# Token halves of the decay logs on the partition halves, zeroing in bf16, and a reordered plan in the recurrent mixer of a four-layer model

## What is computed

```
proj = h @ w_in
qp, fp, ip, gp = split(proj)                       # 1024 columns each
log_f = logaddexp(log(lb), log1p(-lb) + log_sigmoid(fp))
k = (1 - lb) * sigmoid(-fp)
q = silu(qp) * 128 ** -0.5
# per head, with b the running sum of log_f over the tokens:
#   o_n = sum over m <= n of (q_n . (exp(b_n - b_m) * k_m)) v_m
o = o * rsqrt(mean(o * o) + eps) * norm_g * sigmoid(gp)
out = o @ w_out
```

## Time and profile before

| | us |
|---|---|
| median of 3 runs | 1396.22 |
| lowest and highest | 1389.8 and 1397.57 |
| the profiled execution | 1391.12 |
| its span, first to last instruction | 1389.3 |
| PE busy in it | 1338.4 (96%) |
| chain that ended last, on PE | 88% |

### The profile page before, as it was taken

One profiled execution on the slowest core, in us unless ns is written; L12 is line 12 of the kernel. 1 busy time (PEld: TensorE's weight loads), 2 busy tenths in 40 slices (PEclk: granted clock), 3 DMA queues, 4 the chain that ended last, 5 costly groups with the idle time before them and its releaser, 6 DMA issues.

```text
span 1389.3 us, 19642 instructions
## 1 busy us (share of the span) xinstructions
PE 1338.4 (96%) x7598; PEld 1098.7 (79%) x7598; DVE 394.4 (28%) x817; ACT 713.0 (51%) x1241; POOL 1044.5 (75%) x875
## 2 busy tenths in 40 slices
PE   6999899999999999999999998899999999899997
PEld 4888788888877777888887777688887788788886
DVE  2156321111156562211104463301103232411112
ACT  6364564454486765544434564444534554444531
POOL 6244878887894637888888776888879977788874
PEclk9799999999999999999999999999999999999999
DMA  8223456665653423655665543466656544465652
GB/s 270 90 77 92 136 166 199 182 192 173 190 169 92 132 77 122 195 184 182 183 194 160 184 135 122 148 214 186 196 175 190 188 144 152 136 214 182 196 170 89
DMA packets 63116, 224.91 MB, mean 162 GB/s; under 512 B 7344, under 2 KB 7984, under 8 KB 63024
## 3 DMA queue, kind: packets, MB, share of 16 engines
q1 hardware_dynamic: 62736, 223.57, 51.6%
q10 hardware_dynamic: 288, 0.10, 0.0%
HBM read 222.59 MB, written 1.05 MB: 161 GB/s over the span
## 4 chain that ended last, share of the span: by engine, by line
PE 88%; POOL 3%; DVE 3%; ACT 3%; DMA 2%; issue 2%; SPq 0%; DVEq 0%; ACTq 0%
PE G L1027 25%; PE G L1028 24%; PE G L1034 24%; POOL wlo L2168 3%; PE A L1206 1%; PE A L1058 1%; ACT whi L1909 1%; PE A L1140 1%; DMA raw<-in_w_e 1%; PE G L1206 1%; PE A L1272 1%; DMA raw<-in_w_b 1%; PE A L1176 1%; DVE X L1416 1%; PE G L1140 1%
## 5 line engine op out<-in xcount | busy, mean ns | idle before, releaser
L2168 POOL TENSOR_TENSOR wlo<-raw,whi 128x256 fp32r<-128x256 f32 (+1 forms) x867 | 1034.8, 1230 | 326.9 <-ACT whi L1909 326.8
L1909 ACT ACTIVATE whi<-raw 128x1024 fp32r<-128x1024 f32 x403 | 425.7, 1060 | 352.8 <-PE G L1034 325.3
L1027 PE MATMUL G<-whi,xh 128*128 128x512 f32 (+2 forms) x1200 | 465.2, 391 | 9.9 <-DVE xl L1391 6.7
L1028 PE MATMUL G<-whi,xl 128*128 128x512 f32 (+2 forms) x1200 | 452.2, 380 | 0.0
L1034 PE MATMUL G<-wlo,xh 128*128 128x512 f32 (+2 forms) x1200 | 353.4, 381 | 1.6 <-POOL wlo L2168 1.4
L1027 PEld LDWEIGHTS G<-whi,xh 128*128 128x128 f32 x1200 | 228.3, 190 | 54.3 <-ACT whi L1909 8.8
L1028 PEld LDWEIGHTS G<-whi,xl 128*128 128x128 f32 x1200 | 228.8, 191 | 37.7
L1034 PEld LDWEIGHTS G<-wlo,xh 128*128 128x128 f32 x1200 | 220.2, 190 | 46.9 <-POOL wlo L2168 3.6
L1027 PE MATMUL G<-whi,hh 128*128 128x512 f32 x352 | 139.5, 396 | 0.0
L1028 PE MATMUL G<-whi,hl 128*128 128x512 f32 x352 | 138.9, 395 | 0.0
L1034 PE MATMUL G<-wlo,hh 128*128 128x512 f32 x352 | 110.5, 395 | 0.0
(11 more groups left out here) (360 smaller groups left out, 1183.9 us busy)
## 6 DMA issues: line engine op xcount, KB each, us to landing
raw<-in_g SPq DMA_DIRECT2D x88, 512.0 KB, 4.0
raw<-in_u SPq DMA_DIRECT2D x88, 512.0 KB, 4.0
raw<-in_d SPq DMA_DIRECT2D x88, 512.0 KB, 4.2
raw<-in_w_h SPq DMA_DIRECT2D x32, 512.0 KB, 3.6
raw<-in_w_e SPq DMA_DIRECT2D x24, 512.0 KB, 3.8
raw<-in_w_a SPq DMA_DIRECT2D x24, 512.0 KB, 3.6
...
```

What stands on the lines that cost most here:

```text
L1027: e.matmul(o, sh[:, kt, xs], whi[h][:, ws], start=u.first and j == 0, stop=False)
L1028: e.matmul(o, sl[:, kt, xs], whi[h][:, ws], start=False, stop=False)
L1909: e.activation(whi[c % NH][:, 0:n], raw[c % NR][:, 0:n], ACT.Copy).then_inc(s_hi, 1)
L2168: m = e.tensor_tensor(wlo[c % NH][:, i:j], raw[c % NR][:, i:j], whi[c % NH][:, i:j].bitcast(F), ALU.subtract)
```

## The change

**Layout of the logs.** `lfh` and `lfl` become `lf[0]` and `lf[1]`, one for each half of 64 of the 128 tokens. The high part of a token half stays on its own 64 partitions, the low part goes to the other 64. One matmul then contracts high and low part together, but of one token half only. `Wr` keeps its 1152 columns and holds for each token half the three blocks that need whole 128 columns, and, shared by both, the 64-column pieces of the six finer levels. H1 for t = 1 becomes per half 256, 2x64 and 4x64 columns, for t = 0 128, 128, 2x64 and 4x64. FG has two copies of 64 rows for one of 128, FJ two subtractions for one.

**Zeroing in bf16.** A new tile `ZB` of one row and 128 columns in bf16, zeroed once, takes the place of the fp32 row, and the wait for `CN` goes.

**The query gate in PSUM.** FB writes its second clamp to PSUM; its exponential moves from FE to FA (FA has 5 activations for 4, FE 3 for 4), and the last factor lies in PSUM when FF reads it.

**The plan.** Most steps of stage 2 between units 16 and 67 stand at other units, and lanes are given out otherwise. All steps remain; the feed, POOL's and SP's queues and the other stages stay.

```diff
-        lfh = sb("lfh", [128, 2, 512], R, e1)
-        lfl = sb("lfl", [128, 2, 512], R, e1)
+        lf = [sb(f"lf{i}", [128, 2, 512], R, e1) for i in range(2)]
+        ZB = sb("ZB", [1, 128], B16, e1)
...
-                pieces = ((128, 640, 0), (640, 1152, 512)) if t else ((0, 128, 0), (256, 640, 128), (640, 1152, 512))
-                for part, l in enumerate((lfh, lfl)):
-                    for c0, c1, o0 in pieces:
-                        m = e.matmul(tile[:, o0:o0 + c1 - c0], l[:, t, lh], Wr[:, c0:c1],
-                                     start=part == 0 and o0 % 512 == 0, stop=part == 1, skip_group_check=True)
+                for half in range(2):
+                    l, w0 = lf[half][:, t, lh], 384 * half
+                    for c0, c1, o0 in ((0, 256, 0),) if t else ((256, 384, 0), (128, 256, 128)):
+                        e.matmul(tile[:, o0:o0 + c1 - c0], l, Wr[:, w0 + c0:w0 + c1], start=half == 0 and o0 == 0,
+                                 stop=half == 1, skip_group_check=True)
+                    for c0, n, o0 in ((768, 2, 256), (896, 4, 512)):
+                        m = e.matmul(heads4(tile[:, o0:o0 + 128 * n], n)[:, :, 64 * half:64 * half + 64], l,
+                                     heads4(Wr[:, c0:c0 + 64 * n], n), start=half == 0 and o0 == 512, stop=True,
+                                     skip_group_check=True)
...
-                none = CN[0:1, C_CM:C_CM + 128]
-                e.wait_ge(d_cn, 16)
-                e.matmul(tile[:, 0:128], none, none, start=True, stop=False, skip_group_check=True)
+                e.matmul(tile[:, 0:128], ZB[:, :], ZB[:, :], start=True, stop=False, skip_group_check=True)
...
-                e.tensor_scalar(q_, fq, -1.0, 80.0, ALU.mult, ALU.min).then_inc(S["FB"], 1)
+                e.tensor_scalar(L, fq, -1.0, 80.0, ALU.mult, ALU.min).then_inc(S["FB"], 1)
...
-                e.scalar_tensor_tensor(out=fq, in0=fq, scalar=-(128 ** -0.5), in1=q_, op0=ALU.mult,
+                e.scalar_tensor_tensor(out=fq, in0=fq, scalar=-(128 ** -0.5), in1=m, op0=ALU.mult,
...
-                e.tensor_tensor(lfl[:, :, lc], L, lfh[:, :, lc].bitcast(F), ALU.subtract)
+                for half in range(2):
+                    own_, other = slice(64 * half, 64 * half + 64), slice(64 - 64 * half, 128 - 64 * half)
+                    e.tensor_tensor(lf[half][other, :, lc], L[own_], lf[half][own_, :, lc].bitcast(F), ALU.subtract)
...
-                e.activation(lfh[:, :, lc], heads4(tile[:, 0:512], 2), ACT.Copy)
+                for half in range(2):
+                    rows = slice(64 * half, 64 * half + 64)
+                    e.activation(lf[half][rows, :, lc], heads4(tile[rows, 0:512], 2), ACT.Copy)
...
-24: FE 1; H3 0 1; H4 0 0; EV 2 1; FF 1; H4 0 1; HA 0 0
-25: HA 0 1; H5 0 0; FG 1; H5 0 1; H1 1 0 @1; GB 0 @0
+25: FE 1; H3 0 1; H4 0 0; EV 2 1; FF 1; H4 0 1; HA 0 0
+26: HA 0 1; H5 0 0
+27: FG 1; H5 0 1; GB 0 @1; H1 1 0 @0; GC 0; FJ 1
```

More of the change, by code:

```diff
@@ L111, in shape_constants, with level @@
     hm = np.zeros((128, 6, 32), np.float32)
-    hw[:, 0] = s > n
-    hw[:, 1] = s <= n
-    for i, L in enumerate(LEVELS):
+    def level(L):
         mid = n // (2 * L) * 2 * L + L - 1
-        right = n % (2 * L) >= L
-        hw[:, 2 + i] = np.where(right, (s > mid) & (s <= n), (s > n) & (s <= mid))
+        return np.where(n % (2 * L) >= L, (s > mid) & (s <= n), (s > n) & (s <= mid))
+    for half in range(2):
+        for i, m in enumerate((s <= n, level(LEVELS[0]), s > n)):
+            hw[:, 3 * half + i] = np.tile(m[64 * half:64 * half + 64], (2, 1))
+    within = hw[:, 6:9].reshape(128, 6, 64)
+    for i, L in enumerate(LEVELS[1:]):
+        within[:, i] = np.tile(level(L)[0:64, 0:64], (2, 1))
     m, n = s % 32, np.arange(32)[None, :]
@@ L367 @@
 14: FF 0
[L368 to L373, removed]
-24: FE 1; H3 0 1; H4 0 0; EV 2 1; FF 1; H4 0 1; HA 0 0
-25: HA 0 1; H5 0 0; FG 1; H5 0 1; H1 1 0 @1; GB 0 @0
[L376 to L409, removed]
+16: EV 1 1; FG 0; FB 1 @2
+18: FA 1; FJ 0
+19: T1 0 @0; EV 2 0; FD 1; H1 0 0 @1; TV 0
+20: TA 0
+22: H1 0 1 @0
+23: H2 0 0
+24: H2 0 1; H3 0 0
@@ new lines @@
+25: FE 1; H3 0 1; H4 0 0; EV 2 1; FF 1; H4 0 1; HA 0 0
+26: HA 0 1; H5 0 0
+27: FG 1; H5 0 1; GB 0 @1; H1 1 0 @0; GC 0; FJ 1
+29: GF 0; H2 1 0; H1 1 1 @2; T1 1 @1; H2 1 1; H3 1 0
+30: H3 1 1; H4 1 0; TA 1; H4 1 1; H5 1 0
+31: H5 1 1; HA 1 0; HA 1 1; TV 1; EV 3 0; H1 2 0 @0; EV 3 1; H1 2 1 @2; H2 2 0
+32: H2 2 1; H3 2 0; H1 3 0 @1
+33: H3 2 1; H2 3 0; H4 2 0; H3 3 0; H4 2 1; HA 2 0; H5 2 0; FB 2 @0; H4 3 0; HA 2 1; H5 2 1; FA 2
+34: H5 3 0; H1 3 1 @2
+35: HA 3 0; FD 2; H2 3 1; O1 0 @1; FE 2; H3 3 1; EV 4 0; FF 2; H4 3 1; O2 0
@@ new lines @@
+36: HA 3 1; H5 3 1
+37: FG 2; O3 0
+38: FJ 2; MT 0 @2
+39: MH 0; T1 2 @1; ML 0; H1 4 0 @0; TV 2; TA 2; H1 4 1 @2
+41: H2 4 0; H1 5 0 @1; H2 4 1; H3 4 0
+42: H2 5 0
+43: H3 4 1; EV 4 1; H4 4 0; H3 5 0; EV 5 0; H4 4 1; H5 4 0; HA 4 0; GB 1 @0; H4 5 0; GC 1; H5 4 1
+44: H5 5 0; HA 4 1; GF 1; HA 5 0; H1 5 1 @2; O1 1 @1; H2 5 1; H3 5 1
+45: O2 1; H4 5 1; O3 1
+46: HA 5 1; H5 5 1; MT 1 @0
+47: MH 1
+48: EV 5 1; ML 1; FB 3 @1
+49: FA 3
+51: FD 3
+52: EV 6 0; FE 3
+54: FF 3
+56: EV 6 1; FG 3; GB 2 @2; O1 2 @0; GC 2; FJ 3
@@ L410 @@
+57: O2 2; GF 2; T1 3 @1
+58: TV 3; TA 3; H1 6 0 @2
+59: O3 2
+60: H2 6 0; H1 6 1 @1; EV 7 0; H3 6 0; H1 7 0 @0; H2 6 1
+61: H3 6 1; H4 6 0; H2 7 0; H4 6 1; H3 7 0; HA 6 0; H5 6 0; H4 7 0; H5 6 1; HA 6 1; H1 7 1 @1; H5 7 0; HA 7 0
+62: H2 7 1; MT 2 @0; H3 7 1
+63: MH 2; H4 7 1; EV 7 1; ML 2; GB 3 @0
+64: H5 7 1; HA 7 1; GC 3; O1 3 @1; GF 3
+65: O2 3
 66: O3 3
-67: MT 3 @1
+67: MT 3 @0
 68: MH 3
@@ L1697, in bound_begin @@
                 e.wait_ge(d_hn, 48)
+                e.memset(ZB[:, :], 0.0)
                 e.tensor_tensor(w[0][:, :], lb, lb, ALU.subtract)
@@ L2050, in forget_softplus @@
                 _, u = key
-                tile, _ = lane_of("FB", key)
-                L, m = heads4(tile[:, 0:512], 2), heads4(tile[:, 512:1024], 2)
+                tile, w = lane_of("FB", key)
+                L, m, q_ = tile[:, 0:512], tile[:, 512:1024], w[0][:, 0:512]
+                l_ = w[0][:, 512:1024]
                 e.wait_ge(S["FB"], nth("FB", *key))
-                e.activation(L, both_halves(2, 1024 * (u % 3) + 256), ACT.Abs).then_inc(s_act, ac.up())
-                e.activation(m, m, ACT.Exp)
+                e.activation(heads4(l_, 2), both_halves(2, 1024 * (u % 3) + 256), ACT.Abs)
+                e.activation(q_, L, ACT.Exp)
+                e.activation(m, m, ACT.Exp).then_inc(s_act, ac.up())
                 own()
-                e.activation(L, L, ACT.Exp, scale=-1.0).then_inc(s_act, ac.up())
+                e.activation(l_, l_, ACT.Exp, scale=-1.0).then_inc(s_act, ac.up())
                 own()
-                e.activation(L, L, ACT.Ln, bias=1.0).then_inc(S["FA"], 1)
+                e.activation(L, l_, ACT.Ln, bias=1.0).then_inc(S["FA"], 1)
             def forget_logs(key):
@@ L2063, in forget_logs @@
                 m, q_, l_ = tile[:, 512:1024], w[0][:, 0:512], w[0][:, 512:1024]
-                e.activation(q_, q_, ACT.Exp).then_inc(s_act, ac.up())
+                e.activation(q_, q_, ACT.Ln, bias=1.0)
+                e.wait_ge(S["FA"], nth("FA", *key))
+                e.wait_ge(S["FD"], nth("FD", *key))
+                e.activation(l_, m, ACT.Ln, bias=1.0).then_inc(s_act, ac.up())
                 own()
[L2066 to L2070, removed]
+                e.activation(m, q_, ACT.Exp, scale=-1.0).then_inc(S["FE"], 1)
             def forget_hi(key):
```

## The result

| | before | after |
|---|---|---|
| median of 9 runs each, us | 1396.22 | 1387.19 |
| lowest and highest | 1389.49 and 1403.23 | 1384.74 and 1390.82 |
| profiled execution, and its span | 1391.12, 1389.3 | 1384.74, 1382.9 |

The medians are 9.0 us apart. The ratio of the runs (estimated over all of them, so it is not the quotient of the medians) is 0.9943, 95% interval 0.992 to 0.9966: faster by 5 to 11 us, small but clear of the noise. Beside a later group of runs the changed kernel stood at 0.9898, interval 0.9859 to 0.9937. Several terms behind it are wrong all the same, and one cause of the median's move is not in the prediction at all.

What follows compares the result with a forecast made beforehand. PE, 96% busy and 88% of the chain, was taken to bound the kernel. The sum -3.8 - 4.4 + 0.5 - 5.3 + 2.5 = -10.5 us, off the median 1396.2, gave 1385.7; range 1378 to 1391.

Steps and rivals of the forecast that it cites:

- H1: Decay-sum matmuls on PE in stage 2, 16 times: fewer columns save 0.24 us each, -3.8 us.
- zeroing: PE's row of zeros, 16 times: one bf16 pass for two fp32 passes saves 0.27 us each, -4.4 us.
- FG and FJ, T1 0: One instruction more each on ACT and DVE per pair; only pair 0 is waited for, T1 0 0.5 us later: +0.5.
- old waits: PE's waits before H1 1 0 and H1 5 1 and two for EV go or shrink under the new order: -5.3 us.
- new waits: Where four heads stand close, units 29 to 36 and 58 to 63, PE waits 0.3 to 0.7 at five points: +2.5 us.
- All others within 1 us: A sign to look for: stage 2 is 10 to 11 us shorter, every other stage within 1 us.
- loads set PE's pace: Rival, chance 0.07: H1's narrow matmuls each need their whole load row, 0.19 us; H1 gives +5.0, time 1394.5.
- the zeroing is a wait: Rival, chance 0.06: the 0.41 is mostly PE turning from wide to small matmuls; bf16 saves 0.02 each, time 1389.8.
- The order: New plan of stage 2's steps: old waits give -5.3 us, new waits cost +2.5.
- serial clusters: Rival, chance 0.07: ACT's and DVE's work in the two four-head clusters cannot overlap, +14.2 us, time 1402.7.
- the waits did not move in full: Rival, chance 0.20: as many new waits come in the two clusters as old ones go; sum -7.7, time 1388.5.
- The query gate: Last factor in PSUM shortens line 1740, 1.31 against 0.69 us; on PE's path only where H5 waits; no gain counted.

Runs made afterwards that it cites:

- e1_zero: The kernel before with the zeroing in bf16 alone, old plan and old decay sums: median 1393.8 us, ratio 0.9968 beside the kernel before.
- e5_early: The changed kernel with FG 0 and FJ 0 one to three units earlier, at unit 15: median 1382.0 us, ratio 0.9909 beside the kernel before.
- e8_no_gate: The changed kernel with the query gate's clamp and factor back in SBUF: median 1390.6 us, ratio 0.9964 beside the kernel before.
- e4_plan_oldcode: The kernel before, its code unchanged, with the new table of steps for stage 2: median 1387.7 us, ratio 0.9931 beside the kernel before.
- e3_code_oldplan: The changed kernel with the old table of steps for stage 2: median 1394.9 us, ratio 0.9979 beside the kernel before.
- e2_halves: The kernel before with the logs laid out by token halves alone, old order, gate and zeroing: median 1396.5 us, ratio 0.9997 beside the kernel before.
- e7_gate: The kernel before with only the query gate's clamp and last factor in PSUM and its exponential moved: median 1390.8 us, ratio 0.9963.
- c2_after: The changed kernel run once more, unchanged, in a later group: median 1383.6 us, ratio 0.9898 beside the kernel before.

## Why the prediction held, and where it did not

The prediction's sum was -10.5 us in the profiled execution; stage 2 gave -6.9, the whole execution -6.4. Term by term, from the profile after:

| term | predicted | measured | from |
|---|---|---|---|
| H1 | -3.8 | -3.1 | 16.5 to 13.4 |
| zeroing | -4.4 | -4.2 | 0.26 in each H4 |
| FG and FJ, T1 0 | +0.5 | +1.0 | wait 1.5 to 2.5 |
| old waits | -5.3 | -5.3 | all four gone (0.14 left of H1 1 0's, counted below) |
| new waits | +2.5 | +3.4 | 1.3 outside H4; 2.0 inside |
| low clock behind T1 0 | none | +1.5 | window 406.96 to 409.94 |

They add to -6.7, against -6.9. "All others within 1 us" failed too, by the 2.7 and 3.2 outside the stage.

- **H1 and the zeroing** came nearly as priced: 0.70 for "0.68 to 0.75" with t = 1, 0.91 for "0.88 to 0.95" with t = 0 in most, 1.01 and 1.18 in the first two, and 0.16 for "0.10 to 0.16". That the output lies in runs of 64 columns cost little, as assumed. The price of the zeroing had a slip: 0.057 + 0.10 is 0.157, not 0.14, and so 0.25 each and -4.0, where I wrote 0.27 and -4.4; the row measured 0.16. The rival "loads set PE's pace" is refuted by these rows, and "the zeroing is a wait" by e1_zero. By the issue gap that I quoted from the Trainium skill, "TensorE: Matmul & The Clock Gate", Back-to-back issue gap, H1 with t = 1 would have gained nothing; it went from 0.92 to 0.70, and the measurement decides.
- **T1 0** was mis-sized. The step said "FG ends at about 405.4" in before's time and FJ some 0.6 longer. The timelines of ACT and DVE in the profile after show another order of things:

```profile
399.41 1.06 ACT L1920 ACTIVATE whi<-raw 128x1024 fp32r<-128x1024 f32 x1 [1.35 <-DMA raw<-in_w_h]
400.37 0.67 ACT L1933 ACTIVATE PJ<-G,SM 128x512 f32<-128x512 f32 x1
400.94 1.19 ACT L2093 ACTIVATE lf<-A 64x512 fp32r<-64x512 f32 x2
402.03 0.58 ACT L2094 ACTIVATE A<-W 128x512 f32<-128x512 f32 x1
```
```profile
402.72 1.39 DVE L1760 TENSOR_TENSOR lf<-A,lf 64x512 fp32r<-64x512 f32 x2 [0.36 <-ACT A L2094]
404.12 0.69 DVE L1761 SCALAR_TENSOR_TENSOR PJ<-HN,A 128x512 f32<-128x512 f32 x1
```

  ACT stood 1.35 us for a transfer into `raw`, then had a split and EV 1 1 ahead of FG 0, and DVE waited for FG 0's end; FJ's two subtractions took 1.39. The bound, +1.1, held the wait. "The other pairs have 1 us or more between FJ and T1" was wrong for pair 2, whose T1 waited 0.43 for FJ. That a longer wait would also bring down PE's clock stood nowhere; e5_early shows both gone together.
- **The waits of the old order** went, but the first not for the reason named. I wrote that H1 1 0 opens A0, "which TA 0 and TV 0 freed long before". In the new table H1 0 1 has A0 in between (unit 22), so the lane is not T1 0's any more, and H1 1 0 still waits for an H5, that of H1 0 1, which ended at 422.81, 0.05 before H1 1 0 began (DVE's timeline of the kernel after):

```profile
420.52 0.68 DVE L1749 SCALAR_TENSOR_TENSOR PJ<-PJ,G 128x512 f32<-128x512 f32 x1
...
422.31 0.50 DVE L1821 TENSOR_REDUCE DG<-W 128x32 f32<-128x192 f32 x1
```

  The wait fell from 1.88 to 0.14, not to nothing. The unit that now stands between covers 1.4 of it; the shorter line 1749 ahead of that H5 has a part too. With the same order and the old gate it is 1.5 in e8_no_gate and 1.0 in e4_plan_oldcode, where that instruction took 1.54 and 1.55. "That wait goes anyway" did not hold without the gate.
- **New waits** were expected between steps, "0.3 to 0.7 at five points". Outside H4 there are four, 1.3 in all; H1 5 1's 0.4 was not among them. But inside H4 PE lost 2.0 (21.2 where 23.3 - 4.2 = 19.2 was due), 1.4 of it in the two entries "issue", which no step of the prediction has. It was lost at the three places where three H4 stand in a row: they took 4.1, 4.8 and 3.8 us, where 3.5 is the least in e1_zero and e3_code_oldplan. The 4.8 is heads 4 and 5, at unit 43, outside the two places that the prediction looked at. The "issue" waits recur at these places, 0.3 to 1.3 each, in all six other profiles with the new order (one of the two in e4_plan_oldcode), and single ones of 0.5 to 0.9 inside H4 in e1_zero, e2_halves and e3_code_oldplan, but not in e7_gate nor in the two profiles of the kernel before. What PE waits for there stays open: the profile names nothing, and no run tried it.
- **The order** was worth more than its -5.3 + 2.5 = -2.8. e3_code_oldplan against c2_after and after puts 8 to 9 us of stage 2 on the table of steps, about 6 of it beside the low clock (10.2 us for 6.8 and 3.4, half of it lost); the 9 sets the slowest of ten executions against the fastest of nine. The sum had left H1 5 1's wait in the old order at 1.9; with the edits it was 3.4. On the old code, in e4_plan_oldcode, the order lowered the median by 10.6 (interval 4.9 to 14.5), with a stage 2 that was 5 longer in its one profile; why it is worth so much there is not shown. Of the rivals, "serial clusters" did not happen, and the waits did not move in full, 3.4 new ones for 5.3, though stage 2's 6.9 is nearer to that rival's 7.7 than to 10.5.
- **The query gate** is the step that failed most plainly: "shortens line 1740 ... it is on PE's path only where H5 waits behind it". That took 1.31 as the cost of the old form, from one execution. In four kernels with the old form it is 10.6, on the path to T1 0, and in a second profile of this one 2.6, on the path to H1 1 0; how often the kernel before has the 10.6 only its list of runs suggests. e7_gate, the gate alone, gave 0.9963, clear of 1.
- **The median.** I took the sum off the median, 1396.2, as if the 5.1 us between it and the profile were the same noise for both kernels. The changed kernel's profile lies only 2.45 below its median. So it fell 6.4 in the profile and 9.0 in the median, and these 2.6 hid the better part of the 4.1 by which the sum was too large: the right number came from two errors of opposite sign, and that is luck. That the 2.6 are the shut-out's is argued from the spreads and from e7_gate (0.4 in its profile's stage 2, 4.4 in its median), not counted execution by execution.

The four single parts do not add up: 4.5, 1.8, 4.4 and 10.6 us of median in their groups make 21, the whole 9 to 11. Each was timed against a kernel with the other waits still in it; the parts were timed in different groups, the intervals reach 4 to 5 us to either side, and of e2_halves's 1.8 it can't be told whether it is more than nothing.
